# RMS norms squared chunk by chunk on ScalarE, their root taken on one column per token, and the borders of the expert stage prepared earlier

## The reference

```python
def rmsnorm(x, g):
    x32 = x.astype(jnp.float32)
    y = x32 * lax.rsqrt(jnp.mean(x32 * x32, axis=-1, keepdims=True) + NORM_EPS)
    return (y * g.astype(jnp.float32)).astype(x.dtype)
...
h = modulate(rmsnorm(x, ln1_g[l]), sh1, sc1)       # h * (1 + scale) + shift, from c
x = x + g1 * mix(h)                                # RWKV-7, RWKV-7, RG-LRU, latent attention
h2 = modulate(rmsnorm(x, ln2_g[l]), sh2, sc2)
x = x + g2 * peer_ffn(h2, ...)
```

## Time and profile before

| | |
|---|---|
| median of 3 runs | 4443.0 us (4442.14 to 4447.75) |
| the profiled execution | 4449.47 us, its span 4447.4 us |
| busy of the span | PE 92%, PEld 83%, DVE 70%, ACT 54%, POOL 2% |
| HBM | 745.5 MB read, 168 GB/s over the span |
| chain that ended last | PE 81%, DVE 11%, issue 4%, ACT 3%, DMA 1% |
| mean granted clock of PE | 0.973 |

### The profile page before, as it was taken

How to read it: one execution, slowest core, us unless ns; L and a number is a source line. 1 busy time by engine, 2 the same in 40 slices (tenths; PEclk the granted TensorE clock), 3 DMA queues, 4 the chain that set the end, 5 groups by cost and what they waited for, 6 DMA issues and landing times.

```text
span 4447.4 us, 84244 instructions
## 1 busy us (share of the span) xinstructions
PE 4091.9 (92%) x30026; PEld 3701.5 (83%) x30026; DVE 3128.2 (70%) x5181; ACT 2393.5 (54%) x3981; POOL 95.8 (2%) x182
## 2 busy tenths in 40 slices
PE   5889997899998999789988999969999999987998
PEld 5889997777898999767777999957777799986777
DVE  6758857877565886787756678497776678768555
ACT  4146657544433665754445566484443466566444
POOL 0000000000000000000000000000000000000000
PEclk8999999999999999999989999999998999999999
DMA  7345551687513555258743455508883245532554
GB/s 266 111 128 175 180 179 57 198 283 250 164 50 121 175 175 180 75 171 284 258 146 114 157 177 178 169 24 283 284 282 125 88 159 176 179 117 66 190 192 146
DMA packets 203620, 748.59 MB, mean 168 GB/s; under 512 B 22704, under 2 KB 23856, under 8 KB 202192
## 3 DMA queue, kind: packets, MB, share of 16 engines
q1 hardware_dynamic: 178416, 646.51, 43.7%
q0 software_dynamic: 25056, 100.15, 7.5%
HBM read 745.52 MB, written 1.05 MB: 168 GB/s over the span
## 4 chain that ended last, share of the span: by engine, by line
PE 81%; DVE 11%; issue 4%; ACT 3%; DMA 1%; DVEq 0%; ACTq 0%; SPq 0%
PE ps L1842 14%; PE ps L1843 14%; PE ps L1844 14%; PE ps L2260 11%; PE ps L2262 11%; PE ps L2261 11%; DVE t_lo L1705 3%; PE ps L1961 2%; DVE oh L1710 2%; DVE t_lo L1041 1%; DVE arena L1716 1%; ACT t_hi L612 1%; PE ps L1874 1%; PE ps L2213 1%; PE ps L1858 1%
## 5 line engine op out<-in xcount | busy, mean ns | idle before, releaser
L1041 DVE TENSOR_TENSOR t_lo<-raw,t_hi 128x1024 fp32r<-128x1024 f32 x1180 | 1444.6, 1225 | 1095.9 <-ACT t_hi L612 1072.8
L612 ACT CAST t_hi<-raw 128x1024 fp32r<-128x1024 f32 x1180 | 1237.6, 1050 | 1565.7 <-PE ps L1844 805.1
L1842 PE MATMUL ps<-h_hi,t_hi 128*128 128x256 f32 x5344 | 1548.0, 290 | 73.7 <-DVE h_lo L1182 33.8
L1843 PE MATMUL ps<-h_lo,t_hi 128*128 128x256 f32 x5344 | 1525.1, 285 | 0.0
L1844 PE MATMUL ps<-h_hi,t_lo 128*128 128x256 f32 x5344 | 1524.0, 285 | 0.0
L1842 PEld LDWEIGHTS ps<-h_hi,t_hi 128*128 128x128 f32 x5344 | 1036.8, 194 | 99.9 <-issue 73.3
L1843 PEld LDWEIGHTS ps<-h_lo,t_hi 128*128 128x128 f32 x5344 | 1039.4, 195 | 0.8 <-issue 0.5
L1844 PEld LDWEIGHTS ps<-h_hi,t_lo 128*128 128x128 f32 x5344 | 1038.3, 194 | 0.0
L2260 PE MATMUL ps<-t_hi,h_hi 128*128 128x512 f32 x2048 | 815.1, 398 | 16.3 <-DVE t_lo L1041 16.0
L2262 PE MATMUL ps<-t_hi,h_lo 128*128 128x512 f32 x2048 | 802.4, 392 | 0.0
L2261 PE MATMUL ps<-t_lo,h_hi 128*128 128x512 f32 x2048 | 801.0, 391 | 0.0
(11 more groups left out here) (275 smaller groups left out, 2873.8 us busy)
## 6 DMA issues: line engine op xcount, KB each, us to landing
raw<-u_tiles SPq DMA_DIRECT2D x512, 512.0 KB, 3.3
raw<-v_tiles SPq DMA_DIRECT2D x512, 512.0 KB, 4.2
raw<-w_tiles SPq DMA_DIRECT2D x188, 512.0 KB, 3.7
oh<-w_tiles POOLq DMA_DIRECT2D x160, 512.0 KB, 4.8
arena<-w_tiles SPq DMA_DIRECT2D x16, 512.0 KB, 3.7
arena<-keys_t POOLq DMA_DIRECT2D x4, 1024.0 KB, 5.0
arena<-mla_w POOLq DMA_DIRECT2D x1, 4096.0 KB, 14.0
arena<-lora POOLq DMA_DIRECT2D x2, 1280.0 KB, 8.5
```

The costliest lines, as they stand in the source:

```text
L612: act.copy(t_hi[:, j % SPL, :], raw[:, j % RAW, :]).then_inc(hi_done, 1)
L1041: tts(t_lo[:, j % SPL, :], raw[:, j % RAW, :], t_hi[:, j % SPL, :].bitcast(F32), ALU.subtract).then_inc(lo_done, 1)
L1842: mm(o, hi[:, c, :], h_hi[:, c, :], start=(c == 0), stop=False)
L1843: mm(o, hi[:, c, :], h_lo[:, c, :], start=False, stop=False)
```

## The change

Norms. ACT squares each chunk of `x` as soon as it is written; where the norm follows output products, this happens between their tiles. PE takes the squares as the stationary operand and one column of ones as the moving one, so that the sums of a token half stand in one column, a token on each partition (`row_squares`: 2 matmuls of 128 x 1 a chunk, done between the output tiles from the fifth on, and behind the last). ACT's root takes epsilon and 1/1024 itself and works on 128 x 2, as does DVE's reciprocal. PE spreads the result again over all partitions by a product with the identity (`spread_rows`, 2 matmuls of 128 x 128), and DVE reads it from PSUM.

Column sums. At the end of the expert stage only the group of the scale is summed (one instead of two); the group of the shift follows after `spread_rows`, and DVE adds its bias after four chunks (`late`); the third group (two in layer 3) is summed behind the first tile of the input products. POOL's DMAs still wait for that group.

Borders of the expert stage. ACT's and DVE's split of the first `u` tiles goes ahead of the score copies. The first two groups of one-hots are made before the last `u` tiles are used, in the `t_lo` buffer that is free then, and the first group's products no longer wait until PSUM of the last `u` tile is read (the banks are exchanged for that). The first `v` tile is split before the last gate. In turn, in every norm but the first the second tile of what follows is split on DVE behind all eight `h_lo` instead of ahead.

```diff
-GATE_BANKS = [0, 6]
+GATE_BANKS = [6, 0]
...
+            def uppers_and_squares(name, then):      # ACT
+                first, count = SEGS[name][:2]
+                for k in range(2, count):
+                    upper(first + k, first + k, None, name)
+                    if k >= 3:
+                        act.wait_ge(taken, TAKEN[name] + k - 2)
+                        square_of(k - 3)
+                upper(first + count, first + count, None, then)
+                for c in range(count - 3, count):
+                    act.wait_ge(taken, TAKEN[name] + c + 1)
+                    square_of(c)
...
+            def square_of(c):
+                act.activation(wide[:, c, :], x[:, c, :], ACT.Square).then_inc(squares, 1)
...
-                seen(ms_ready)
-                act.activation(rinv_all, ms_all, ACT.Sqrt).then_inc(root, 1)
+                seen(sumsq)
+                act.activation(root_of_row, row_sums(bank), ACT.Sqrt, scale=1.0 / D, bias=eps[:, 0:1]).then_inc(root, 1)
...
                 distances(0)                         # ACT, odd_hots
-                for m in range(n):
+                last_two(KEYS - 2)
+                weights(0)
+                last_two(KEYS - 1)
+                distances(1)
+                for m in range(1, n):
...
-                link(dve.reciprocal(rinv_all, rinv_all))          # DVE
+                dve.reciprocal(rinv_of_row, root_of_row).then_inc(rinv_rows, 1)
...
+                before = 4 if late else 2
                 for c in range(DC):
+                    if late and c == before:
+                        late()
                     scaled_by(wide, gain, c, normed)
...
+                if then != "dq":
+                    lower(first + 1, first + 1, then)
...
                 dve.wait_ge(sel_ready, TT * (l + 1))              # DVE, gates
+                columns(0, 0)
+                columns(1, 1)
+                dve.wait_ge(tile_used, first + KEYS - 1)
+                rows(0, 0).then_inc(hot, 1)
+                dve.wait_ge(tile_used, first + KEYS)
+                rows(1, 1).then_inc(hot, 1)
                 dve.wait_ge(taken, TAKEN[f"u{l}"] + KEYS)
...
+                lower(SEGS[f"v{l}"][0], SEGS[f"v{l}"][0], f"v{l}")
                 seen(gates_t)
                 gate(n - 1, 1)
...
+            def row_squares(c, bank=2):                           # PE
+                seen(squares)
+                for tt in range(TT):
+                    ins = mm(ps[:, bank + 2 * tt, 0:1], wide[:, c, tt * P:(tt + 1) * P], ones[:, 0:1], start=(c == 0),
+                             stop=(c == DC - 1))
...
+            def spread_rows():
+                seen(rinv_rows)
+                for tt in range(TT):
+                    ins = mm(ps[:, 2, tt * P:(tt + 1) * P], rinv_of_row[:, tt:tt + 1].broadcast_to([P, P]), ident,
+                             start=True, stop=True)
...
+            def products_and_squares(name):
+                products(name, 0, 4, fresh=True)
+                for k in range(4, DC):
+                    products(name, k, k + 1)
+                    row_squares(k - 4)
+                for c in range(4, DC):
+                    row_squares(c)
...
-                products("dkv", fresh=True)
+                products("dkv", 0, 1, fresh=True)
+                late_sums(3, AT_TAIL, IN_NORM[3], 5)
+                products("dkv", 1)
...
-                seen(score_out, 4)
+                seen.skip(score_out, 4)
...
                 gate(0)
+                pe.wait_ge(taken, TAKEN[f"u{l}"] + KEYS)
                 gate(1)
```

More of the change, by code:

```diff
@@ L372, in build, with hot_rows @@
         wa_hi, wa_lo = h_hi, h_lo
-        hot_rows = [t_lo[:, b, :].rearrange("p (q k) -> p q k", q=8) for b in range(2)]
+        def hot_rows(l, b):
+            return t_lo[:, (SEGS[f"u{l}"][0] + b) % SPL, :].rearrange("p (q k) -> p q k", q=8)
         hot_cols = [v[:, :, :, :].rearrange("p a q k -> p (a q) k") for v in (oh1, oh2)]
@@ L1069, in add_products @@
                     take_out(k, (first + k) % 2).then_inc(taken, 1)
+                    if k == count - 2:
+                        lower(first + count, first + count, then)
                 dve.wait_ge(taken, TAKEN[name] + count)
@@ L1183, in lower_of, with norm @@
                         .then_inc(h_split, 1)
+                before = 4 if late else 2
                 for c in range(DC):
+                    if late and c == before:
+                        late()
                     scaled_by(wide, gain, c, normed)
-                    if c >= 2:
-                        lower_of(c - 2)
-                lower_of(DC - 2)
-                lower_of(DC - 1)
-            def norm(g, scale, shift, then):
+                    if c >= before:
+                        lower_of(c - before)
+                for c in range(DC - before, DC):
+                    lower_of(c)
+            def norm(g, scale, shift, then, begun=False, late=None):
+                first = SEGS[then][0]
                 if then == "dq":
                     ahead(then)
-                else:
-                    statistics(then)
-                if then == "dq":
                     modulation(3, [0, 1], 5, IN_NORM[3])
+                elif not begun:
+                    lower(first, first, then)
                 link(stt(gain[:, :], scale, 1.0, g, ALU.add, ALU.mult))
-                modulated(shift)
+                if then != "dq":
+                    inverse_root()
+                    seen(rinv_wide)
+                modulated(shift, late)
+                if then != "dq":
+                    lower(first + 1, first + 1, then)
             def split_lower():
@@ L1710, in hots @@
                         ins = ts(hot_cols[b][:, q, :], iota, col(1), col(2), ALU.is_equal, ALU.mult)
-                    ins.then_inc(hot, 1)
+                    return ins
+                def hots(m, b):
+                    rows(m, b)
+                    columns(m, b).then_inc(hot, 1)
                 def gate(m, b):
@@ L1746, in step @@
                 def step(n, j, k, i):
-                    lower(n, j, name)
+                    if j > first:
+                        lower(n, j, name)
                     lower_gated(k + 1, j - first + 1, i, j + 1)
@@ L1792, in _ @@
                 if l == 3:
-                    norm(pcol("kv_g"), mod_kv[:, 8:16], mod_kv[:, 0:8], "dkv")
+                    norm(pcol("kv_g"), mod_kv[:, 8:16], mod_kv[:, 0:8], "dkv", late=last_turned(3))
                     attention()
@@ L2284, in _ @@
             for l in range(4):
-                sum_squares(wide, DC)
+                for c in range(DC):
+                    row_squares(c, 4 if l == 2 else 2)
+                spread_rows()
                 if l == 0:
```

238 lines of the change are left out of this document (135 added, 103 removed).

## The result

The changed kernel takes **4402.9 us** (median of 4 runs, 4396.1 to 4407.9) against 4445.4 for the kernel before it (4 runs, 4442.1 to 4453.0): ratio 0.9896, 95% interval 0.9882 to 0.991. It is faster, as forecast, by 42.5 us and not by 63. The profiled execution's span fell from 4447.4 to 4401.4. Both numbers lie inside the recorded range; all four runs are above the forecast of 4380.

A forecast was written before the change was run, and what follows sets the result against it. PE, busy 92% of the span, was taken as the bound, so only its idle or half-clock time could be gained. Terms summed to 62.9 us off the profiled 4449.5, giving 4386.6, or a median of 4380; range 4358 to 4408.

The forecast's parts named there:

- First `u` product: Start of the `u` stage, four layers: PE's 2.96 wait and most half clock behind it go; 4.4 each, 17.6 us.
- way to the gates: Last `u` product to second gate, four layers: two one-hot groups made ahead leave this path; 4.0 each, 16 us.
- Rival (c): `u` stage: choosing takes back the gain if DVE's queue sets the pace, leaving 1.5 a layer; 4392 us, chance 0.10.
- Start of the `v` stage: Last gate to first `v` tiles, four layers: earlier split shortens the way, a fold's DMA wait limits it; 5.3 us gained.
- Second norms: Norm ahead of the query products, four layers: shorter path from squares to first product; 2.2 each, 8.8 us.
- (a): Every norm's border: PE at half clock, norms give 3.1 instead of 22.5; 43.5 in all, 4400 us, chance 0.20.
- (b): Norms and layer borders: full clock throughout, 77 us gained in all, 4366 us, chance 0.12.
- layer borders: Norms between layers: 3.2 us gained from layer 0 to 1, 9 from 1 to 2, -1.5 from 2 to 3.
- Layer 2 to 3: Border into layer 3: column sums behind the first tile and late `positions` outweigh the shorter norm; -1.5 us.
- Rival (d): Six norms: a table switch holds ACT about its load's 1.28 again, root 1.2 later; 4387 us, chance 0.05.
- Rival (e): Gate stage: clock falls and stays, 3.9 instead of 3.26 us a group, slower at 4457 us, chance 0.04.

The follow-up runs named there:

- e3: Kernel before the change with only the expert stage's part of the change added, its norms untouched; 4427.2 us, ratio 0.9943 to the kernel before.
- e4: Changed kernel with the expert stage's part taken out again, leaving the norms' part alone; 4433.6 us, ratio 0.9942 to the kernel before.
- e10: Changed kernel with GpSimd issuing the DMAs for the first folds of layers 0 to 2 earlier, folds left in place; 4387.7 us, ratio 0.9859.
- e5: Changed kernel with only the first fold of layers 0 to 2 one tile later on VectorE; 4391.6 us, ratio 0.9852 to the kernel before.
- e7: Changed kernel with products that nobody reads keeping TensorE busy at each layer's second norm; 4402.3 us, ratio 0.9873 to the kernel before.
- e8: Changed kernel with first fold later, late column sums ahead of the first tile, and layer 3's last 32 sums in the attention's idle gap; 4377.5 us, ratio 0.9830.

## Why the prediction was right, and what it had wrong

- **Direction and mechanism: right.** Where PE idles at the borders is where the time was, and the parts add up (e3 and e4).
- **First `u` product and way to the gates: right**, 19.6 and 15.2 for 17.6 and 16. Rival (c) did not come: the gain of the `u` start is still there in the last `u` tiles, within 0.2 in each layer.
- **Start of the `v` stage: the step that failed**, 5.3 forecast, -6.9 measured. The first `v` product came as counted, 1.04 behind the last gate's end in every layer instead of 2.74. In layers 0 to 2 the prediction had the wait right (a fold that waits for its DMA, PE idle ahead of the second tile) and two sizes in it wrong. It took the DMA's 4.05 us over from the earlier trace rows unchanged; the fold starts 6.0, 4.6 and 6.9 behind the gate now, 4.9 us more in all than before. And it had the second tile at full clock, as it was; it takes 4.4, 4.3 and 5.2 us instead of 2.7 to 2.8, 5.6 more in all. That is 10.5 of the 10.7 missed there (2.1 forecast, -8.6 measured). In layer 3 (3.2 forecast, 1.7 measured) it is the clock too: the 1.4 counted for a first tile at full clock did not come, the tile takes 4.4 us, where in e3, behind the same idle 2.3, it takes 2.8. The late landing goes with a `v` tile's load that the earlier `t_lo` of the first tile sets free (e3 against e4). The prediction counted the DMA of the fold and not this one. e10 takes the landing away, e5 what stands behind it; by the ratios they return 11 and 14 us.
- **Mixing stages: no term at all, -12.3 measured.** Of it 6.0 is the half clock in layer 3's attention, which comes with the norms. The rest, in layers 0 and 1, goes from -3.7 to +1.2 between profiles of kernels that are alike there. e3, whose mixing stages are those of the kernel before, has -1.7 and -2.5 there. So it is not assigned to the change.
- **Second norms: 8.8 forecast, 13.5 measured.** In layer 0 it was 10.2 us from the last `out` product to the first query product (253.56 to 263.79) and is 6.1 (255.06 to 261.16): 4.1, and 4.5 to 4.6 in the other layers, for the 4.4 counted. The sums between the tiles, three groups, took 0.9 and not 1.4: the tiles around them are 3.32 us apart, and 3.03 on average before. But the 0.8 for the second tile's `t_lo` was not lost: PE idles 0.60 ahead of it (267.02), in a tile that `h_lo` paces anyway (e7).
- **Rivals (a) and (b) went by the clock and missed.** Full clock throughout, (b), did not come. (a)'s condition came true: half clock at all four second norms and over 20.5 us between layers 1 and 2. Its price did not: norms, layer borders and end gave 13.5 + 8.5 + 4.7 = 26.7 with it, where (a) had 3.1 and the forecast 22.5 without the start. The time of 4400 that it names came out of other terms.
- **Layer 2 to 3: -1.5 forecast, -3.6 measured.** The column sums take 4.03 behind the first tile, for 3.63 counted. DVE's wait for `positions` is there, 6.60 us, but PE has no gap ahead of the fourth tile. The four tiles, without the sums, take 16.7, where the kernel before had 13.7 (3368.75 to 3382.49). They are at half clock from 3328.2 to 3333.2 and from 3336.6 to 3343.5, and before for 3.4 us in all.
- **Rival (d), the drain behind a table load, did not come.** ScalarE in layer 3's second norm:

```profile
3489.77 0.42 ACT L667 ACTIVATE arena<-x 128x256 f32<-128x256 f32 x1 [2.11 <-DVE x L1126]
3490.20 1.28 ACT L678 ACT_TABLE_LOAD   x1
3491.49 0.26 ACT L678 ACTIVATE by_row<-ps,eps 128x2 f32<-128x2 f32 x1
```

The load stands between square and root, and the root starts 0.01 behind it. So it is in five of the six norms; in the last the root starts 0.70 behind the load, and waits for PE's sums. The Trainium skill's "ScalarE: Activation LUTs", section "What ACT_TABLE_LOAD costs", adds some 1380 ns there; this row has no such time.
- **Rival (e) did not come**: it decides from 3.8 us a group on, and from the second group on VectorE's gates are 3.29 apart, in both kernels. The 3.26 of the prediction is a mean that takes in the last step, which is shorter (2.22). The first gate starts at 696.29, 2.0 behind the end of the last `u` product at 694.25, as asked; before it was 6.2 (701.40 to 707.62).

## What to carry to other kernels

When a step is made earlier, follow what it frees as well as what it makes: the buffer that it reads comes free earlier, the next load starts earlier, and a transfer that was alone on the DMA engines may not be any more. An instruction that waits for a DMA should have nothing behind it in its queue that the busiest engine needs soon; one place further down was worth 14 us here. And before a price is put on PE's half clock, see whether PE is what paces the stretch: three of four such stretches were taken away for nothing.

## What was not expected of the hardware

- One DMA of 512 KB, issued at the same point of the program, was there 4.1 to 4.3 us behind the last gate in six of six stages without the early split of a `v` tile (before, e4) and 4.6 to 6.9 in nine of nine with it (e3 and the changed kernel's two profiles). The `v` tile's load ran within that time in all nine and in none of the six. What sets the spread from 4.6 to 6.9 was not found.
- The clock's half stretch over the end of layer 3's attention (17 us) follows the same instructions and the same idle 2.9 us that in e3 are followed by 3.4 us, and stays for 10.3 us with the idle time filled (e8). What sets it was not found.
